# Router products with the router's weights stationary, shares ahead of the gathered rows, first gather in two banks

## What is computed

```python
# block 1: h = rms_norm(x, norm2_g) * (1 + sc2) + sh2
g_prob = softmax(h @ w_group + b_group);  g_p, g_idx = top_k(g_prob, 1)
e_p, e_idx = top_k(softmax((h @ w_expert + b_expert) of the group), 2)
w = g_p * e_p / sum(e_p)
out[token] += w * ((silu(h @ w_gate[e]) * (h @ w_up[e])) @ w_down[e])
# block 2
top_logits, top_e = top_k(h @ w_router + b_router, 4);  top_w = softmax(top_logits)
gu = h @ w_gu[e] + b_gu[e];  act = (clip(lin) + 1) * (glu * sigmoid(1.702 * glu))
out[token] += top_w * (act @ w_dn[e] + b_dn[e])
```

## Time and profile before

| | |
|---|---|
| three runs, us | 2140.18, 2142.71, 2146.76 |
| median | 2142.71 |
| the profiled execution | 2141.7 |
| its span, first to last instruction | 2139.9 |
| mean granted TensorE clock | 0.947 |
| TensorE, PEld, DVE, ACT busy | 88%, 50%, 25%, 18% |
| from HBM | 624.39 MB, 292 GB/s |

### The profile page before, as it was taken

One profiled execution on the slowest core, in us unless ns is written; L12 is line 12 of the kernel. 1 busy time (PEld: TensorE's weight loads), 2 busy tenths in 40 slices (PEclk: granted clock), 3 DMA queues, 4 the chain that ended last, 5 costly groups with the idle time before them and its releaser, 6 DMA issues.

```text
span 2139.9 us, 28358 instructions
## 1 busy us (share of the span) xinstructions
PE 1885.5 (88%) x10935; PEld 1070.9 (50%) x10938; DVE 538.6 (25%) x1231; ACT 385.6 (18%) x875; POOL 44.5 (2%) x107
## 2 busy tenths in 40 slices
PE   6999999976686779999988999888998999988895
PEld 4664678854444466677753443333333344333333
DVE  3675332121111223232421111111111111111112
ACT  3232452021110110243120111111110111110012
POOL 0030000000000200100000000000000000000000
PEclk9999899988888889899978999999998999999998
DMA  9969622319999712233342999999999599999993
GB/s 399 370 232 358 240 79 88 149 36 417 418 418 387 272 43 79 67 92 102 142 169 112 416 418 417 416 416 418 417 417 401 241 417 418 416 417 417 418 417 152
DMA packets 108344, 626.77 MB, mean 293 GB/s; under 512 B 11168, under 2 KB 15264, under 8 KB 49792
## 3 DMA queue, kind: packets, MB, share of 16 engines
q1 hardware_dynamic: 106112, 618.81, 71.5%
q0 software_dynamic: 1584, 4.33, 1.1%
q10 hardware_dynamic: 560, 2.35, 0.3%
HBM read 624.39 MB, written 1.05 MB: 292 GB/s over the span
## 4 chain that ended last, share of the span: by engine, by line
PE 59%; DMA 21%; SPq 11%; issue 3%; DVE 3%; ACT 2%; DVEq 0%; ACTq 0%
PE ps L452 56%; DMA ring<-in_w_gu_dram 14%; SPq L501 6%; SPq L504 5%; DMA ring<-in_moe_w_gate_dram 4%; PE ps L569 3%; DMA ring<-in_ada_w_dram 1%; ACT arena L1344 1%; DMA ring<-in_moe_w_down_dram 1%; DMA ring<-in_w_mod_dram 1%; SPq L474 0%; DVE rstd L1735 0%; DVE arena L2099 0%; PE ps L815 0%; SPq L411 0%
## 5 line engine op out<-in xcount | busy, mean ns | idle before, releaser
L452 PE MATMUL ps<-ring,arena 128*64 128x512 f32 (+2 forms) x5248 | 918.4, 564 | 126.7 <-issue 54.5
L452 PEld LDWEIGHTS ps<-ring,arena 128*64 128x64 f32 (+1 forms) x5248 | 293.5, 131 | 692.2 <-issue 501.5
L452 PE MATMUL ps<-arena 64*128 64x256 f32 (+10 forms) x1762 | 263.0, 378 | 31.9 <-ACT arena L1344 15.9
L452 PE MATMUL ps<-hT,ring 128*128 128x256 f32 (+1 forms) x960 | 237.0, 402 | 2.3 <-DVE hT L1781 2.3
L452 PEld LDWEIGHTS ps<-arena 64*128 64x128 f32 (+6 forms) x1764 | 155.6, 164 | 136.4 <-issue 76.4
L452 PEld LDWEIGHTS ps<-hT,ring 128*128 128x128 f32 x960 | 180.3, 192 | 58.8 <-issue 33.7
L2125 DVE TENSOR_SCALAR arena<-ps 128x512 f32<-128x512 f32 x34 | 23.5, 692 | 549.9 <-PE ps L452 549.9
L1344 ACT ACTIVATE arena<-ps 128x256 f32<-128x256 f32 (+4 forms) x195 | 107.3, 574 | 291.3 <-PE ps L452 150.3
L1608 ACT ACTIVATE arena<-ps,mod,gain 128x128 f32<-128x128 f32 x180 | 67.7, 458 | 435.2 <-PE ps L452 435.2
L452 PE MATMUL ps<-arena,hN 128*128 128x128 f32 (+1 forms) x960 | 129.0, 294 | 15.4 <-DVE arena L2075 9.0
L452 PEld LDWEIGHTS ps<-arena,hN 128*128 128x128 f32 x960 | 120.0, 205 | 40.8 <-issue 16.7
(11 more groups left out here) (257 smaller groups left out, 920.1 us busy)
## 6 DMA issues: line engine op xcount, KB each, us to landing
ring<-in_w_gu_dram SPq DMA_DIRECT2D x256, 1024.0 KB, 20.0
ring<-in_w_dn_dram SPq DMA_DIRECT2D x128, 1024.0 KB, 23.3
ring<-dense_dram SPq DMA_DIRECT2D x56, 1024.0 KB, 10.6
ring<-in_moe_w_gate_dram SPq DMA_DIRECT2D x32, 1024.0 KB, 12.7
ring<-in_moe_w_up_dram SPq DMA_DIRECT2D x32, 1024.0 KB, 19.1
ring<-in_moe_w_down_dram SPq DMA_DIRECT2D x32, 1024.0 KB, 18.1
ring<-in_ada_w_dram SPq DMA_DIRECT2D x24, 1024.0 KB, 18.3
ring<-in_w_mod_dram SPq DMA_DIRECT2D x24, 1024.0 KB, 8.6
```

Source lines behind the costliest of these rows:

```text
L452: ins = nc.tensor.matmul(*a, start=start, stop=stop, **k)
```

## The change

- `router`: the router's weights (36 or 32 columns) are stationary and xT's 256 tokens move. The results lie as rows, router outputs on partitions 0 to 35 (or 31) and the sum of squares, made with one column of ones stationary, on partition 96, all in columns 0 to 255 of bank 1. A zero product in bf16 over all 128 partitions opens the bank.
- `router_turn`, new: DVE copies the 128x256 rows to `rows` (a free part of `rstd`), TensorE turns the two halves back into bank 1, and only then come the variance and the turnings of xT. The place counts move to columns 256 and up.
- Block 1: DVE makes shares and spread list before it waits for the gather and rescales.
- Block 2: the first gather's halves go to banks 0 and 3 with no wait between them; ScalarE rescales the first, DVE the second, after its shares and spread list.

```diff
@@ -198,6 +198,7 @@
         gqk = tab[:, 800:928].rearrange("p (a b) -> p a b", b=HD)
         rb = tab[0:1, 928:996]
         rstd = sb("rstd", [P, 2 * T])
+        rows = rstd[:, T:2 * T]
         ARENA = 16100
         arena = sb("arena", [P, ARENA])
         ps = ctx.enter_context(nc.psum_tensor("ps", [P, 8, 512], F32))
@@ -866,17 +867,22 @@
 
                 wr, nr = routers[n][0:2]
                 pe.wait_ge(madeV, nth(madeV, ("xf", n, c)))
+                if c == 0:
+                    mm(ps[:, 1, 0:T], zero16[:, 0:P], zero16[:, 0:T], start=True, stop=False, skip_group_check=True)
                 for k in (2 * c, 2 * c + 1):
-                    for tt in range(TT):
-                        mm(ps[:, 1, tt * 64:tt * 64 + nr], xT[:, k, tt * P:(tt + 1) * P], wr[:, k, :],
-                           start=k == 0 and tt == 0, stop=False, skip_group_check=True)
+                    mm(ps[0:nr, 1, 0:T], wr[:, k, :], xT[:, k, :], start=False, stop=k == KD - 1, skip_group_check=True)
                 pe.wait_ge(madeA, nth(madeA, ("sq", n, c)))
                 for k in (2 * c, 2 * c + 1):
-                    for tt in range(TT):
-                        last = mm(ps[:, 1, 128 + tt:129 + tt], hT[:, k, T + tt * P:T + (tt + 1) * P], ones[:, 0:1],
-                                  start=False, stop=k == KD - 1, skip_group_check=True)
+                    last = mm(ps[96:97, 1, 0:T], ones[:, 0:1], hT[:, k, T:2 * T], start=False, stop=k == KD - 1, skip_group_check=True)
                 if c == 3:
-                    last.then_inc(filled, mark(filled, ("router", n)))
+                    last.then_inc(filled, mark(filled, ("router rows", n)))
+
+            def router_turn(n):
+
+                pe.wait_ge(madeV, nth(madeV, ("rows", n)))
+                for tt in range(TT):
+                    last = transpose(ps[:, 1, tt * P:(tt + 1) * P], rows[:, tt * P:(tt + 1) * P])
+                last.then_inc(filled, mark(filled, ("router", n)))
 
             gate_at = [0, None]
             gate_keys = [(x, c) for c in range(4) for x in ("mga", "mgs")] + [(x, c) for c in range(4) for x in ("ga2", "gb2")]
@@ -967,6 +973,7 @@
 
             def moe_front(n):
 
+                router_turn(n)
                 for j, bank in enumerate((0, 2, 3, 4)):
                     tt, q = j // 2, j % 2
                     for k in range(4):
@@ -977,11 +984,11 @@
 
                 pe.wait_ge(madeV, nth(madeV, ("chosen", n)))
                 for tt in range(TT):
-                    mm(ps[:, 1, 128 + tt * E:128 + (tt + 1) * E], cst("before"), Am[:, tt, :], start=True, stop=tt == 0)
+                    mm(ps[:, 1, 256 + tt * E:256 + (tt + 1) * E], cst("before"), Am[:, tt, :], start=True, stop=tt == 0)
                     if tt == 1:
-                        mm(ps[:, 1, 128 + E:128 + 2 * E], ones, Am[:, 0, :], start=False, stop=True)
+                        mm(ps[:, 1, 256 + E:256 + 2 * E], ones, Am[:, 0, :], start=False, stop=True)
                 for tt in range(TT):
-                    last = mm(ps[0:1, 1, 256:256 + E], ones[:, 0:1], Am[:, tt, :], start=tt == 0, stop=tt == 1)
+                    last = mm(ps[0:1, 1, 384:384 + E], ones[:, 0:1], Am[:, tt, :], start=tt == 0, stop=tt == 1)
                 last.then_inc(filled, mark(filled, ("places", n)))
                 pe.wait_ge(madeA, nth(madeA, ("hN", n)))
                 mm(ps[:, 4, :], zero16[:, 0:P], zero16, start=True, stop=True)
@@ -1002,12 +1009,12 @@
                                   start=tt == 0, stop=tt == 1)
                 last.then_inc(s["gathered"], 1)
 
-            def gather_half(s, onehot, half):
+            def gather_half(s, onehot, half, bank=0):
 
                 for k in range(4):
                     for tt in range(TT):
                         d = (4 * half + k) * P
-                        last = mm(ps[:, 0, k * P:(k + 1) * P], hN[:, tt, d:d + P], onehot[:, tt, :], start=tt == 0, stop=tt == 1)
+                        last = mm(ps[:, bank, k * P:(k + 1) * P], hN[:, tt, d:d + P], onehot[:, tt, :], start=tt == 0, stop=tt == 1)
                 last.then_inc(s["gathered"], 1)
 
             def spread_turn(s, onehot, bank, at):
@@ -1191,9 +1198,7 @@
 
                 pe.wait_ge(s["gather_onehot"], 1)
                 for half in range(2):
-                    if half == 1:
-                        pe.wait_ge(s["xs"], 1)
-                    gather_half(s, ohgF, half)
+                    gather_half(s, ohgF, half, 3 * half)
                 pe.wait_ge(madeV, nth(madeV, ("tables", 2)))
                 run_experts(pe, 2, further, first, begin)
                 pe.wait_ge(s["ys"], E + 1)
@@ -1629,9 +1634,8 @@
                     copy(onehotT, ps[:, 3, T:2 * T] if n == 1 else ps[:, 1, 0:T]).then_inc(s["spread"], 1)
 
                 if n == 2:
-                    for half in range(2):
-                        act_.wait_ge(s["gathered"], half + 1)
-                        half_out(s, half, xsP, 0)
+                    act_.wait_ge(s["gathered"], 1)
+                    half_out(s, 0, xsP, 0)
                 else:
                     act_.wait_ge(s["gathered"], 1)
                     half_out(s, 1, xsP, 2)
@@ -2006,13 +2010,15 @@
             def moe_front(n):
 
                 nr = routers[n][1]
+                v.wait_ge(filled, nth(filled, ("router rows", n)))
+                V.tensor_copy(rows, ps[:, 1, 0:T]).then_inc(madeV, mark(madeV, ("rows", n)))
                 v.wait_ge(filled, nth(filled, ("router", n)))
-                ts(rtok[:, :], ps[:, 1, 128:128 + TT], 1.0 / D, EPS, ALU.mult, ALU.add).then_inc(madeV, mark(madeV, ("var", n)))
+                ts(rtok[:, :], ps[:, 1, 96:96 + P + 1:P], 1.0 / D, EPS, ALU.mult, ALU.add).then_inc(madeV, mark(madeV, ("var", n)))
                 v.wait_ge(madeA, nth(madeA, ("std", n)))
                 V.reciprocal(rtok[:, :], rtok[:, :]).then_inc(madeV, mark(madeV, ("r", n)))
                 v.drain()
                 for tt in range(TT):
-                    last = stt((lg if n == 1 else le)[:, tt, 0:nr], ps[:, 1, tt * 64:tt * 64 + nr], rtok[:, tt:tt + 1],
+                    last = stt((lg if n == 1 else le)[:, tt, 0:nr], ps[:, 1, tt * P:tt * P + nr], rtok[:, tt:tt + 1],
                                constant[:, 0:nr], ALU.mult, ALU.add)
                 step(last)
                 if n == 1:
@@ -2024,13 +2030,13 @@
                 tt_(le[:, :, :], le[:, :, :], each(m8[:, :, 0], E), ALU.subtract).then_inc(madeV, mark(madeV, ("shifted", n)))
                 v.drain()
                 v.wait_ge(filled, nth(filled, ("places", n)))
-                places = ps[:, 1, 128:128 + TT * E].rearrange("p (t e) -> p t e", e=E)
+                places = ps[:, 1, 256:256 + TT * E].rearrange("p (t e) -> p t e", e=E)
                 step(stt(sel[:, :, 0:E], places, 1.0, Am[:, :, :], ALU.add, ALU.mult))
 
             def block_tables(n):
 
                 N = E if n == 2 else E // 4
-                cnt = ps[0:1, 1, 256:256 + E]
+                cnt = ps[0:1, 1, 384:384 + E]
                 c0, c1 = crow[0:1, 0, 0:N], crow[0:1, 1, 0:N]
                 if n == 1:
                     step(V.tensor_reduce(c1, cnt.rearrange("o (p x) -> o p x", x=4), AX.X, ALU.max))
@@ -2100,9 +2106,10 @@
                     last.then_inc(s["xs"], 1)
 
 
-                def pair_out(s, dst):
+                def pair_out(s, dst, half=0, bank=0):
                     for k in range(4):
-                        last = ts(dst[:, k, :], ps[:, 0, k * P:(k + 1) * P], gs[:, k:k + 1], sh[:, k:k + 1], ALU.mult, ALU.add)
+                        d = 4 * half + k
+                        last = ts(dst[:, d, :], ps[:, bank, k * P:(k + 1) * P], gs[:, d:d + 1], sh[:, d:d + 1], ALU.mult, ALU.add)
                     last.then_inc(s["xs"], 1)
 
                 def ys_out(s, dst, dst1):
@@ -2165,12 +2172,13 @@
                 block_tables(n)
                 if n == 2:
                     select(esel16[0], 0)
-                else:
-                    v.wait_ge(s["gathered"], 1)
-                    pair_out(s, xsP)
                 shares(n)
                 spread_onehot(s, ohsF, 0, slots0)
                 v.wait_ge(s["gathered"], n)
+                if n == 1:
+                    pair_out(s, xsP, 0, 0)
+                else:
+                    pair_out(s, xsP, 1, 3)
                 gather_onehot(s, ohgF, n, slots0, n)
                 run_experts(v, n, further, first)
```

## The result

The changed kernel takes 2124.11 us, median of six (2122.43 to 2128.51), against 2141.53 (six, 2137.13 to 2146.76) for the kernel before in the same rounds: a ratio of 0.9921, 95% interval [0.9908, 0.9934]. The forecast was 2135.2, its range 2129.5 to 2142.5. The sign was right and the size was less than half of what came.

A forecast was written before the change was run, and what follows sets the result against it. DMA was taken to bound the second experts, its clock starting with the first expert's products. From 2141.7, second router -6.8 and first -0.7 gave 2134.2, plus 1.0 to the median: 2135.2 us, range 2129.5 to 2142.5.

The forecast's parts named there:

- What bounds the kernel: Second experts limited by DMA, whose clock starts with the first expert's products; router savings before that move the end one for one.
- Second router, products: Block 2: narrow cuts run side by side and the clock rises after 4 to 5 us; saves 7.5 us.
- the passes of the two cuts start in turn: Second router: a stated sign that the forecast is wrong, since it expected both cuts' passes to start together.
- Turn: Second router: DVE's copy, TensorE's turning of two blocks and hand-overs add 1.0 us, bounds 0.9 and 1.3.
- Two banks: Block 2's first gather: both halves back to back, DVE rescaling the second; saves 1.9 us, down to 0.5.
- The clock behind it: Behind the second router: a thin stretch lowers TensorE's clock over the gathers; +2.0 us, bounds -2 and +4.
- First router, products and turn: Block 1: unlike cuts don't overlap and pause at changes, products +1.0 us; the turn another +1.0 us.
- Order: Block 1: shares and spread list made beside the gather, ahead of rescaling; -3.2 us, bounds -2.3 and -3.4.
- The clock term: Block 1's two gathers: each can move a microsecond either way; +0.5 us, bounds -3 and +3.
- The clock holds: Rival: gathers at full clock in both stages, up to 1 us from earlier expert rows; 2132.0 us, chance 0.22.
- Half clock all the way: Rival: in the second router the clock never rises and cuts run in turn; 2146.6 us, chance 0.08.
- less than it says: Rival: sequencer opens both loops, so two banks save 0.5 and the new order 2.3; 2137.5 us, chance 0.10.

The follow-up runs named there:

- a1: Changed kernel with both moves undone (block 1's order, block 2's two banks), leaving only the new router products and turn: 2138.43 us, ratio 0.9992 to the kernel before.
- a4: Changed kernel with block 1's squares over 64 rows, so both kinds of product there use 64-wide cuts: 2122.51 us, ratio 0.9915 to the kernel before.
- b1: Changed kernel with block 1's rescaling of gathered rows put back ahead of the shares: 2131.23 us, ratio 0.9951 to the kernel before.
- a3: Changed kernel with block 2's squares as 64 equal rows, a cut of another width than the router's: 2130.81 us, ratio 0.9957 to the kernel before.
- b2: Changed kernel with block 2's first gather back in one bank and ScalarE alone rescaling: 2130.72 us, ratio 0.9953 to the kernel before.
- a2: Changed kernel with the old router products and no turn in both blocks, new orders and banks kept: 2130.19 us, ratio 0.9954 to the kernel before.
- c2: Kernel before, with 32 waits on a finished load added in TensorE's program ahead of the second router: 2144.36 us, ratio 1.0018 to the unpadded kernel before.
- b4: Changed kernel with the old router products in block 1 alone, all moves kept: 2122.24 us, ratio 0.9919 to the kernel before.

## Why the prediction was right or wrong, point by point

- **What bounds the kernel: right, with a gap.** The end moved with the start of the experts. The step "one for one" failed in block 1: between the two lies the supply of ring slots, and the experts took 3 to 3.7 us longer from their first load on in a1, a4 and b1. That a saving "moves the end by as much" needs the transfers to stay full.
- **Second router, products: right.** Forecast 6.3 us from start to end of the products; 1061.74 to 1067.9 is 6.2. Overlap as assumed, and a3 prices it. The clock rose at 1066.1, some 4.3 us after the start, as forecast. The prediction gave "the passes of the two cuts start in turn" as a sign of being wrong. Their starts do alternate, but the passes overlap; the sign was worded for cuts that run one after another.
- **Turn: right in size.** Copy and two turnings come to 0.95 beside the forecast 1.0. The choice behind it became 1.0 shorter (6.63 to 5.64) rather than 0.4, as that stretch now ran at clock 1.00 (1068.0 to 1074.5).
- **Two banks: right for what it named,** 1.93 for 1.9. It stopped at the bias products; b2 shows 1.70 more in the expert rows.
- **The clock behind it: the term that failed.** I charged +2.0 by analogy with the first stage. Block 2's gathers ran at 1.00 throughout, as before, so the charge is 0. And the row that I read as a low clock at the first expert rows was a credit to be had: their stretch went from 15.73 at 0.88 to 13.83 at 1.00. From +2.0 to -1.9 is 3.9 us. That credit needed both the second bank and the missing hole: the rows take 15.53 with one bank and no hole (a1, b2), and 16.68 with two banks and the hole (a2).
- **The hole: not in the sum at all.** The same row, 1095.60 to 1102.40, shows TensorE busy 4.71 of 6.80 us with nothing to wait for. I read its clock and not its busy time. Without it the rows start 2.67 us sooner. It goes with the position of the code (c2), not with any work: a part of this change's gain is luck, the 2.67 us and, going by a2's rows, the clock's 1.9 as well.
- **First router, products and turn: right in the difference** (+1.97 for +2.0). Both sides of it were set too high: the four pieces take 7.2 us before (7.8 in the prediction, which starts the first at 405.55 where the earlier trace rows has 405.74) and 8.0 after (8.8). The two errors nearly cancel, which is luck. That cuts of 64 and 32 don't overlap is right by after's groups of four; equal ones do (a4).
- **Order: right** (3.3 from the end of the gather for 3.2). The clock term had +0.5: the first gather took 0.55 more, the second 2.2 less (6.02 to 3.84), which takes the new order (b1) and the new router (a2, b4) together. No step of the prediction joins these two.
- **Sum.** Second router -6.8 forecast, -14.2 measured: 3.9 clock, 2.7 hole, 0.6 choice. First: -0.7 forecast, -3.35 measured, mostly the second gather's clock. In the median 17.4 came for 7.5.
- **Rivals.** "The clock holds" named the right mechanism at 2132.0 and was mis-sized: it priced only the gathers and up to 1 us of the rows. "Half clock all the way" fell with the rise at 1066.1, "less than it says" with 5.94 up to the bias products and 3.16 behind the first gather. The range was narrower than my own bounds: with -2 and -3 for the two clock terms the sum is 2127.7. Of the 3.6 us from there down to 2124.1, 1.2 is that the kernel before measured 2141.5 over six runs and not 2142.7; the rest had no term at all, and the hole, 2.67, is enough for it.

## What to carry to other kernels

Before costing a change, add up every idle time behind it until the next long stretch, with "issue" rows among them, and ask of each low clock whether the wait ahead of it is one that the change shortens: a shortened wait was worth 1.7 and 2.4 us more in the work behind it, in two places here (b2, b1), though in neither by itself: the one also needed the hole gone (a2), the other the new router (a2, b4). With stationary weights of few columns, give products that shall overlap cuts of one size, each its own. Where a few microseconds are compared, shift the code by some tens of harmless instructions once: what changes then isn't the edit's.

## What was unexpected of the hardware

- TensorE stands idle for 2.1 us (its weight loads for 3.0) while no weights move, with nothing in the profile to wait for, and the place moves with 32 instructions of padding (c2). In block 1's experts, beside weight transfers at 417 GB/s, such times are 5.3 to 5.5 us, three in before, and 2.7 to 4.5 us, six in after. (Three times of 11.5 to 11.9 us in each are left out: by the chain of waits, weight transfers are part of them.) The q8 packets of the first ones stand 2.6 to 2.9 us ahead of TensorE's next product (487.4 and 490.29, 493.3 and 495.95 in after; 494.8 and 497.74 in before), much as in block 2. The transfers of such a time of after, 491.2 to 496.0 (packets, MB, share):

```profile
q1 hardware_dynamic: 271, 1.97, 99.8%
q8 instruction: 1, 0.02, 1.3%
```

- These idle times cost nothing as long as the transfers stay full: after has 21 us of them and before 16, with equal times from first load to end (251.6 and 251.9).
- Passes of two products whose operands are wholly different overlap when each uses its own cut of one size, and not with cuts of 32 and 64 columns (a3): 0.43 us for two passes of 256 columns at a clock of 0.50, 0.22 at 1.00 (a4's rows).
